# Ten dense matmuls of a recurrent step: two runs of five instead of five short runs

## The chip, the cores and the metric

The kernel runs on one core of a Trainium2 chip. The metric is the time of one execution on the device in microseconds; lower is better.

## The reference

The reference is one layer of a bidirectional encoder for two sequences (1024 and 512 tokens, width 1024), all in float32, with shared weights:

- RMSNorm, then one input projection `u = h @ w_in`. Its columns feed two groups of heads: an RWKV-7 time mixer (8 heads of 64, two directions) and an HGRN2 mixer (4 heads of 128, two directions).
- The RWKV-7 mixer is a recurrence over tokens. The state of each head is a 64 x 64 matrix, `S = S * w + (S @ -kk) b^T + v k^T`, and the output is `y = S @ r`.
- The HGRN2 mixer is a gated linear recurrence in chunks of 32 tokens. Its inputs q, f (two directions), i and g are 20 column tiles of 128 of `u`.
- Both outputs through one output projection, residual, RMSNorm, a mixture of experts (one of 4 groups, then 2 of 8 experts), residual, final RMSNorm.

## The kernel before

The kernel is a row of stages: `norm_in`, `project_rwkv` (the RWKV columns of `u`), **`mix_rwkv_project_hgrn`** (the fused stage, which the change touches), `mix_hgrn`, `mixer_out`, `route`, `experts`, `combine`. Each stage writes one instruction stream for each engine by hand, in program order, with semaphores between them. An engine does its stream strictly in that order, so a wait holds everything behind it. In the code `dve` is VectorE, `act` ScalarE, `pe` TensorE, `sp` the queue that issues most DMAs, `pool` GpSimd.

The fused stage does two jobs at once. One is the RWKV-7 recurrence in 48 chunks of 32 tokens, in both directions at a time. Three chunks are in flight: in a step of number `it`, chunk `a = it` is at its front, `b = it - 1` in the middle, `c = it - 2` at its back. There are 50 steps; 46 of them have all three. The other job is the projection of the HGRN2 columns: 60 units (20 column tiles, 3 spans of 512 tokens) of 8 dense 128x128x512 matmuls each. `project(it, lo, hi)` issues dense matmuls `lo` to `hi` of the ten that belong to a step (L968), so that 48 steps have dense work. Units take turns in two PSUM tiles `pp`, which ScalarE evicts; for the q columns `project` also does four transposes (L976) in the middle of a later unit.

The small groups of TensorE in a step, 16 matmuls each unless said otherwise (each float32 matmul is two records in the profile, so a group of 16 has 32):

- `right(c)` L1008, L1013 (two times 16): the right-hand side R. It waits for the state of the chunk before, for O of the chunk before (ScalarE's copy of the outputs out of the same PSUM tile, L1163), and for the v tile.
- `power` 2, 3 and 4 for `b` and 0 and 1 for `a` (L993, L995, L998): the inverse of a 32x32 triangular matrix by repeated squaring. Between two powers VectorE adds, copies and transposes the result (function `grow` in VectorE's part, L1197, L1199, L1201). The marks `turn1` to `turn4` say that the transpose is done; power i waits for `turn i`, power 0 for `P0`, a transpose of `m0`.
- `solve(c)` L1022, L1025 (two times 16): the solution u and part of the outputs. ScalarE then copies u from PSUM in four pieces (L1137).
- `scores(a)` L985: scores of the new chunk; VectorE masks them, ScalarE makes `m0` of them.
- `grow(c)` L1034, L1038 (two times 16), the function of TensorE's part: growth of the state and the rest of the outputs. It waits for the copies of u. VectorE then makes the new state (L1259, L1262).

TensorE's order in a step was: `right`, 3 dense, power 2, `solve`, `scores`, 2 dense, `grow`, power 3, 2 dense, power 0, 2 dense, power 4, 1 dense, power 1. The last dense matmul and the first three of the next step are parted by power 1 and `right` only. VectorE's order in a step was: work after power 2, masks, state (after `grow`), P0, work after power 3, after power 0, after power 4, after power 1, then what the projection needs of it. ScalarE's order in a step: R, copies of u, copies of the keys, `m0`, logarithms and exponentials of the HGRN2 gates in some steps, O, and evictions of the dense units between them.

## Time and profile before

| | us |
|---|---|
| median of 3 runs | 2946.04 (2942.31 to 2947.09) |
| the profiled execution: its own time | 2947.06 |
| its span, first to last instruction | 2945.3 |
| the fused stage, first dense matmul to last output copy | 592.18 to 1409.50, 817.32 |
| TensorE busy in the stage | 799.61 |
| VectorE busy in the stage | 376.28 |
| ScalarE busy in the stage | 342.79 |

Over the whole span TensorE is busy 82%, VectorE 39%, ScalarE 25%; the mean granted clock of TensorE is 0.891 of 2.4 GHz, in the fused stage 0.98. TensorE is the engine that is almost always busy in this stage, so the table is to be read together with the order of time inside a step: which engine releases TensorE's next group, and how far ahead of time.

### The profile page before, as it was taken

The numbers are of one execution on the slowest core, as the hardware profiler recorded it, in microseconds if no ns is written. First come the engines' busy times: TensorE is split into PE (matmuls) and PEld (weight loads), VectorE is DVE, ScalarE is ACT, GpSimd is POOL, SyncE is SP. The second block draws the span as 40 slices with busy tenths as digits, with TensorE's granted clock in tenths as the row PEclk, the third lists the DMA queues.
The fourth block names the chain that finished last, engine by engine and source line by source line (L and its number), as shares of the span: only waits on it lengthen the run. The fifth ranks groups of instructions, "written<-read, shape, count | busy, mean of one in ns | idle before, by whom it ended". The sixth has DMA issues, their size and how long they took to land. (4 is left out here: it accounts for less than half of the span.)

```text
span 2945.3 us, 64059 instructions
## 1 busy us (share of the span) xinstructions
PE 2405.8 (82%) x27916; PEld 1521.8 (52%) x27916; DVE 1135.2 (39%) x2034; ACT 726.5 (25%) x1362; POOL 198.3 (7%) x272
## 2 busy tenths in 40 slices
PE   3999999499999999999794266884199999999970
PEld 2434333155555555555693023342187888788850
DVE  3128776724634535436552654523010000000006
ACT  3124434423533534435111111110001011011002
POOL 0002111300000000000000000000300100011000
PEclk9999889599999999999796577887599999999985
DMA  3103333423433333332455233325378888888848
GB/s 86 48 8 106 122 103 120 152 69 77 113 83 79 111 83 86 97 83 64 138 157 192 76 110 107 112 81 115 108 302 327 328 327 311 326 330 325 315 154 323
DMA packets 348914, 460.45 MB, mean 156 GB/s; under 512 B 170272, under 2 KB 269200, under 8 KB 340496
## 3 DMA queue, kind: packets, MB, share of 16 engines
q1 hardware_dynamic: 338128, 421.87, 43.4%
q0 software_dynamic: 10560, 35.22, 3.0%
q8 instruction: 184, 3.01, 0.4%
q14 instruction: 42, 0.34, 0.0%
HBM read 348.52 MB, written 108.48 MB: 155 GB/s over the span
## 5 line engine op out<-in xcount | busy, mean ns | idle before, releaser
L968 PE MATMUL m_ps_pp<-hT,h_wcol 128*128 128x512 f32 x960 | 481.9, 623 | 24.2 <-DVE m_decay L1183 24.2
L421 PE MATMUL r_pp<-hT,r_wcol 128*128 128x512 f32 x720 | 314.0, 597 | 14.9 <-DMA r_wcol<-in_w_in_dram 14.6
L968 PEld LDWEIGHTS m_ps_pp<-hT,h_wcol 128*128 128x128 f32 x960 | 163.3, 190 | 158.8 <-issue 120.7
L2146 PEld LDWEIGHTS e_ps_g<-e_xT,e_wg 128*128 128x128 f32 x2048 | 235.6, 193 | 16.3 <-issue 16.3
L2156 PE MATMUL e_ps_y<-e_wd,e_hid 128*128 128x512 f32 x512 | 227.3, 597 | 12.9 <-DVE e_hid L2190 12.9
L2146 PE MATMUL e_ps_g<-e_xT,e_wg 128*128 128x128 f32 x2048 | 235.9, 276 | 1.1 <-DVE e_xT L2185 1.1
L2146 PE MATMUL e_ps_u<-e_xT,e_wu 128*128 128x128 f32 x2048 | 233.9, 275 | 0.0
L421 PEld LDWEIGHTS r_pp<-hT,r_wcol 128*128 128x128 f32 x720 | 137.5, 192 | 185.5 <-issue 185.5
L2146 PEld LDWEIGHTS e_ps_u<-e_xT,e_wu 128*128 128x128 f32 x2048 | 231.3, 192 | 0.0
L2190 DVE TENSOR_TENSOR e_hid<-e_ps_u,e_silu 128x512 f32<-128x512 f32 x32 | 22.1, 692 | 443.5 <-PE e_ps_u L2146 443.5
L1667 PE MATMUL o_ps_out<-o_wout,o_y 128*128 128x512 f32 x384 | 179.0, 627 | 0.0
L2156 PEld LDWEIGHTS e_ps_y<-e_wd,e_hid 128*128 128x128 f32 x512 | 94.7, 190 | 125.2 <-issue 125.2
L1667 PEld LDWEIGHTS o_ps_out<-o_wout,o_y 128*128 128x128 f32 x384 | 78.2, 205 | 101.9 <-issue 99.3
L1137 ACT ACTIVATE m_v<-m_ps_x 32x256 f32<-32x256 f32 x192 | 71.9, 374 | 177.3 <-PE m_ps_x L1025 175.6
L2193 DVE COPY e_y<-e_ps_y 128x512 f32<-128x512 f32 x32 | 22.1, 692 | 217.7 <-PE e_ps_y L2156 217.7
L2136 PE MATMUL e_ps_t<-ident,e_x 128*128 128x128 f32 x264 | 35.7, 279 | 80.8 <-DMA e_x<-h,e_idx 80.8
L2168 ACT ACTIVATE e_xT<-e_ps_t 128x512 f32<-128x512 f32 x33 | 19.7, 597 | 305.6 <-PE e_ps_t L2136 305.6
L1751 DVE RECIPROCAL o_rt<-o_rt 128x512 f32<-128x512 f32 x24 | 80.4, 3348 | 1.5 <-ACT o_rt L1701 0.7
L1649 PE MATMUL o_ps_mean<-o_of,headsum 128*128 128x512 f32 x24 | 23.9, 1099 | 66.0 <-DVE o_of L1728 66.0
L2136 PEld LDWEIGHTS e_ps_t<-ident,e_x 128*128 128x128 f32 x264 | 32.7, 192 | 81.9 <-issue 81.9
L1189 DVE TENSOR_TENSOR m_sm<-m_ps_s,m_mask 128x256 f32<-128x256 f32 x96 | 40.0, 424 | 90.1 <-PE m_ps_s L985 67.0
L2176 ACT ACTIVATE e_y<-e_ps_y 128x512 f32<-128x512 f32 x32 | 19.1, 597 | 219.8 <-PE e_ps_y L2156 219.8
(310 smaller groups left out, 3319.9 us busy)
## 6 DMA issues: line engine op xcount, KB each, us to landing
e_wg<-in_moe_w_gate_dram SPq DMA_DIRECT2D x32, 2048.0 KB, 8.0
e_wu<-in_moe_w_up_dram SPq DMA_DIRECT2D x32, 2048.0 KB, 12.5
e_wd<-in_moe_w_down_dram SPq DMA_DIRECT2D x32, 2048.0 KB, 13.1
ar<-r_ar SPq DMA_DIRECT2D x24, 512.0 KB, 2.7
kb<-r_kb SPq DMA_DIRECT2D x24, 512.0 KB, 2.7
m_ar<-ar SPq DMA_DIRECT2D x48, 256.0 KB, 4.4
m_kb<-kb SPq DMA_DIRECT2D x48, 256.0 KB, 3.5
kq<-h_kqst SPq DMA_DIRECT2D x24, 512.0 KB, 4.2
```

What stands on the lines that cost most here:

```text
L421: last = nc.tensor.matmul(pp[s][:], wcol[q][:, c], self.hT[:, c, s * SPAN:(s + 1) * SPAN], start=c == 0, stop=c == KT - 1)
L968: last = nc.tensor.matmul(pp[n % 2][:], wcol[k % 3][:, c], self.hT[:, c, span(s)], start=c == 0, stop=c == KT - 1)
L1137: last = nc.scalar.activation(out, ps_ru[quad[q]], ACT.Copy)
L1189: nc.vector.tensor_tensor(by_dir(sm[a % RING][:, w::2]), by_dir(ps_s[:, w, :, 0:2 * CH]), mask[:].unsqueeze(2).broadcast_to((P, 2, 2, 2 * ...
L1649: nc.tensor.matmul(ps_mean[:], self.headsum[:], of[u][:], start=True, stop=True).then_inc(*pe_r.inc("mean"))
L1667: last = nc.tensor.matmul(ps_out[:, half * SPAN:(half + 1) * SPAN], y[:, k, t * P:(t + 1) * P], wout[:, k, half * SPAN:(half + 1) * SPAN], ...
L1751: nc.vector.reciprocal(rt[u][:], rt[u][:]).then_inc(*dve_n.inc("inv"))
L2136: last = nc.tensor.transpose(ps_t[:, c * P:(c + 1) * P], x[u][:, c:D:KT], self.ident[:])
L2146: last = nc.tensor.matmul(ps[:, q * P:(q + 1) * P], w[u][:, c, q * P:(q + 1) * P], xT[u][:, c * P:(c + 1) * P], start=c == 0, stop=c == KT ...
L2156: last = nc.tensor.matmul(ps_y[:, n * 512:(n + 1) * 512], hid[u][:, q * P:(q + 1) * P], wd[u][:, q, n * 512:(n + 1) * 512], start=q == 0, ...
L2190: nc.vector.tensor_tensor(hid[u][:], ps_u[:], silu[:], ALU.mult).then_inc(*dve.inc("hid"))
L2193: nc.vector.tensor_copy(y[u][:, 512:], ps_y[:, 512:]).then_inc(*dve.inc("y"))
```

## The change

On TensorE, the ten dense matmuls of a step are issued as two runs of five. Power 2 moves ahead of the first run, power 3 ahead of `grow`, and power 0, power 4 and power 1 stand side by side after the second run, followed by `right` and power 2 of the next step. On VectorE, the work after power 3 moves ahead of the new state. No instruction is added or taken away.

```diff
                         if has_c:
                             right(c)
-                        project(it, 0, 3)
                         if has_b:
                             self.waits(eng, dve_a.at("turn2", b))
                             power(ps_b, b % 2, 2).then_inc(*pe_b.inc("I2"))
+                        project(it, 0, 5)
                         if has_c:
                             solve(c)
                         if has_a:
                             scores(a)
-                        project(it, 3, 5)
-                        if has_c:
-                            grow(c)
                         if has_b:
                             self.waits(eng, dve_b.at("turn3", b))
                             power(ps_b, b % 2, 3).then_inc(*pe_b.inc("I3"))
-                        project(it, 5, 7)
+                        if has_c:
+                            grow(c)
+                        project(it, 5, 10)
                         if has_a:
                             self.waits(eng, dve_a.at("P0", a))
                             power(ps_a, a % 2, 0).then_inc(*pe_a.inc("I0"))
-                        project(it, 7, 9)
                         if has_b:
                             self.waits(eng, dve_b.at("turn4", b))
                             power(ps_b, b % 2, 4).then_inc(*pe_b.inc("I4"))
-                        project(it, 9, 10)
                         if has_a:
                             self.waits(eng, dve_a.at("turn1", a))
                             power(ps_a, a % 2, 1).then_inc(*pe_a.inc("I1"))
...
                             masked(a, 1)
+                        if has_b:
+                            self.waits(eng, pe_b.at("I3", b))
+                            grow(dve_b, ps_b, b, 4)
                         if has_c:
...
-                        if has_b:
-                            self.waits(eng, pe_b.at("I3", b))
-                            grow(dve_b, ps_b, b, 4)
                         if has_a:
                             self.waits(eng, pe_a.at("I0", a))
                             grow(dve_a, ps_a, a, 1)
```

TensorE in the fused stage before, from power 1 of one step to power 3 of the next (a row is a line, its operation, tile written <- tiles read, the moving tile, and a count; `m_ps_a` and `m_ps_b` are the powers of chunks a and b, `m_ps_pp` the dense units):

```order
L995 MATMUL m_ps_a<-m_px,m_pw 32x64 x16
L1008 MATMUL m_ps_x<-m_v,m_sm 32x64 x16
L1013 MATMUL m_ps_x<-m_state,m_ar 32x64 x16
L968 MATMUL m_ps_pp<-hT,h_wcol 128x512 x3
L995 MATMUL m_ps_b<-m_px,m_pw 32x64 x16
L1022 MATMUL m_ps_x<-m_rs,m_xt 32x64 x16
L1025 MATMUL m_ps_x<-m_ar,m_state 64x32 x16
L985 MATMUL m_ps_s<-m_ar,m_kb 64x128 x16
L968 MATMUL m_ps_pp<-hT,h_wcol 128x512 x2
L1034 MATMUL m_ps_x<-m_v,m_kbt 64x64 x16
L1038 MATMUL m_ps_x<-m_sm,m_v 64x32 x16
L995 MATMUL m_ps_b<-m_px,m_pw 32x64 x16
```

The same place now, from power 0:

```order
L993 MATMUL m_ps_a<-m_m,m_pw 32x32 x16
L998 MATMUL m_ps_b<-m_px,m_pw 32x32 x16
L995 MATMUL m_ps_a<-m_px,m_pw 32x64 x16
L1008 MATMUL m_ps_x<-m_v,m_sm 32x64 x16
L1013 MATMUL m_ps_x<-m_state,m_ar 32x64 x16
L995 MATMUL m_ps_b<-m_px,m_pw 32x64 x16
L968 MATMUL m_ps_pp<-hT,h_wcol 128x512 x5
L1022 MATMUL m_ps_x<-m_rs,m_xt 32x64 x16
L1025 MATMUL m_ps_x<-m_ar,m_state 64x32 x16
L985 MATMUL m_ps_s<-m_ar,m_kb 64x128 x16
L995 MATMUL m_ps_b<-m_px,m_pw 32x64 x16
L1034 MATMUL m_ps_x<-m_v,m_kbt 64x64 x16
```

Power 0 (L993), 4 (L998), 1 (L995 of `m_ps_a`), `right` and power 2 follow each other without a dense matmul between them, and so do solve, scores, power 3 and `grow`.

VectorE before, from the masks of a step to the work after power 0 (`m_ps_b` rows belong to power 3, the line `m_grown` to the state):

```order
L1189 TENSOR_TENSOR m_sm<-m_ps_s,m_mask 128x4x64 x2
L1259 TENSOR_TENSOR m_grown<-m_ps_x,m_state 128x2x4x64
L1262 TENSOR_TENSOR m_state<-m_grown,m_decay 128x512
L1267 STREAM_TRANSPOSE m_pw<-m_m 128x128
L1268 TENSOR_TENSOR m_px<-m_m,m_eye 128x4x32
L1197 TENSOR_TENSOR m_px<-m_px,m_ps_b 128x4x32
L1199 COPY m_px<-m_ps_b 128x4x32
L1201 STREAM_TRANSPOSE m_pw<-m_px 128x128
L1199 COPY m_px<-m_ps_a 128x4x32
```

The same place now (its lines stand three higher up to the masks, L1189 is L1186):

```order
L1186 TENSOR_TENSOR m_sm<-m_ps_s,m_mask 128x4x64 x2
L1194 TENSOR_TENSOR m_px<-m_px,m_ps_b 128x4x32
L1196 COPY m_px<-m_ps_b 128x4x32
L1198 STREAM_TRANSPOSE m_pw<-m_px 128x128
L1259 TENSOR_TENSOR m_grown<-m_ps_x,m_state 128x2x4x64
L1262 TENSOR_TENSOR m_state<-m_grown,m_decay 128x512
L1267 STREAM_TRANSPOSE m_pw<-m_m 128x128
L1268 TENSOR_TENSOR m_px<-m_m,m_eye 128x4x32
L1196 COPY m_px<-m_ps_a 128x4x32
```

The three instructions after power 3 moved ahead of the two of the state and of P0.

## Rows read from the trace of the kernel before

**Rows 1.** The page, groups of instructions: busy us, mean ns | idle us before it
```profile
L968 PE MATMUL m_ps_pp<-hT,h_wcol 128*128 128x512 f32 x960 | 481.9, 623 | 24.2 <-DVE m_decay L1183 24.2
```

**Rows 2.** Windows (us): busy us and (x) records of each engine, clock, DMA share, GB/s
```profile
1005.59:1021.89 16.30, 16.30 (x411) 9.46 (x404) 8.21 (x24) 5.92 (x16) 0.00 (x0) 1.00 0.39 110
1153.82:1172.76 18.94, 16.58 (x425) 9.60 (x418) 11.25 (x31) 12.89 (x23) 0.00 (x0) 1.00 0.45 113
1172.76:1189.06 16.30, 16.30 (x408) 9.45 (x413) 10.61 (x27) 10.15 (x20) 0.00 (x0) 1.00 0.30 100
969.99:987.83 17.84, 17.84 (x408) 10.35 (x412) 10.61 (x27) 10.19 (x20) 0.00 (x0) 0.91 0.26 87
969.95:973.30 3.35, 3.35 (x66) 2.09 (x67) 3.28 (x7) 1.55 (x2) 0.00 (x0) 0.50 0.92 329
1372.79:1390.57 17.78, 17.78 (x408) 10.30 (x412) 10.61 (x27) 10.14 (x20) 0.00 (x0) 0.91 0.21 72
```

**Rows 3.** TensorE's waits, 600 to 1390: us in total, times, longest
```profile
PE m_ps_x L1008 <- issue: 9.4, 4, 2.4
```

**Rows 4.** Order of time (start, us, engine line, tiles), TensorE, one step
```profile
1005.98 2.84 PE L968 MATMUL m_ps_pp<-hT,h_wcol 128*128 128x512 f32 x6
...
1008.75 0.65 PE L995 MATMUL m_ps_b<-m_px,m_pw 32*32 32x64 f32 x32
...
1009.17 0.52 PEld L1022 LDWEIGHTS m_ps_x<-m_rs,m_xt 32*32 32x32 f32 x32
...
1009.78 1.06 PE L1025 MATMUL m_ps_x<-m_ar,m_state 64*64 64x32 f32 x30
...
1011.74 1.98 PE L968 MATMUL m_ps_pp<-hT,h_wcol 128*128 128x512 f32 x4
...
1013.65 0.69 PE L1034 MATMUL m_ps_x<-m_v,m_kbt 64*64 64x64 f32 x32
...
1014.71 0.65 PE L995 MATMUL m_ps_b<-m_px,m_pw 32*32 32x64 f32 x32
...
1015.29 1.98 PE L968 MATMUL m_ps_pp<-hT,h_wcol 128*128 128x512 f32 x4
...
1017.21 0.45 PE L993 MATMUL m_ps_a<-m_m,m_pw 32*32 32x32 f32 x32
...
1017.59 1.98 PE L968 MATMUL m_ps_pp<-hT,h_wcol 128*128 128x512 f32 x4
...
1020.94 0.59 PE L995 MATMUL m_ps_a<-m_px,m_pw 32*32 32x64 f32 x27
...
1021.32 0.21 PE L1008 MATMUL m_ps_x<-m_v,m_sm 32*32 32x64 f32 x1
```

**Rows 5.** The same step, ScalarE and VectorE
```profile
1010.95 1.53 ACT L1137 ACTIVATE m_v<-m_ps_x 32x256 f32<-32x256 f32 x4 [4.39 <-PE m_ps_x L1025]
...
1017.74 0.29 DVE L1199 COPY m_px<-m_ps_a 128x128 f32<-128x128 f32 x1 [0.33 <-PE m_ps_a L993]
...
1018.06 0.31 DVE L1201 STREAM_TRANSPOSE m_pw<-m_px 128x128 f32<-128x128 f32 x1
```

**Rows 6.** Order of time, the last steps of the stage
```profile
1390.14 0.59 PE L995 MATMUL m_ps_a<-m_px,m_pw 32*32 32x64 f32 x27
...
1391.75 0.65 PE L995 MATMUL m_ps_b<-m_px,m_pw 32*32 32x64 f32 x32 [0.20 <-DVE m_pw L1201]
...
1392.77 1.12 PE L1025 MATMUL m_ps_x<-m_ar,m_state 64*64 64x32 f32 x32
...
1393.94 1.53 ACT L1137 ACTIVATE m_v<-m_ps_x 32x256 f32<-32x256 f32 x4 [1.88 <-PE m_ps_x L1025]
...
1395.53 0.69 PE L1034 MATMUL m_ps_x<-m_v,m_kbt 64*64 64x64 f32 x31 [1.63 <-ACT m_v L1137]
```

**Rows 7.** Order of time around one late O
```profile
969.48 0.36 ACT L1163 ACTIVATE m_oacc<-m_ps_x 128x256 f32<-128x256 f32 x1
...
969.94 1.08 PE L1008 MATMUL m_ps_x<-m_v,m_sm 32*32 32x64 f32 x32 [2.36 <-issue]
```

## The prediction

> **What bounds the kernel now.** I read the groups of instructions first, then busy time by stretch, then the waits, and last the order of time inside one step. The groups show that the dense matmuls of the fused stage are 481.9 us of TensorE [rows 1], the costliest line of the program; the change moves just these. The windows show one ordinary step of the stage, from the second half of one `right` to that of the next: 16.30 us, and TensorE is busy for all of them at the full 2.4 GHz [rows 2]. So in an ordinary step nothing but TensorE's own queue sets the time: every microsecond of idle that a new order brings is paid, and every drain that it saves is a gain. Four of the 48 `right` groups are an exception: TensorE waits before them, 9.4 us in all [rows 3]. These steps take 18.94 us [rows 2], because ScalarE, 12.89 us busy, is late with its copy of the outputs (O), which `right` waits for: O starts at 969.48, `right` at 969.94 (the row names no releaser, only "issue"; O's end is the last event before it) [rows 7].
>
> **What five runs cost now.** All starts in this paragraph are in [rows 4]. A dense matmul is two records. Six records take 2.77 us until the next small group (1005.98 to 1008.75), four take 1.91 (1011.74 to 1013.65), so a record is 0.43 us and entering a small group from a dense run costs about 0.20 on top. A 32x64 group is 0.42 us when another 32-row group follows (1008.75 to 1009.17, power 2 before solve) and 0.58 when a dense run follows (1014.71 to 1015.29, power 3), so leaving costs 0.16. Each dense run thus costs some 0.36 us beyond its matmuls. A step has five and will have two: 1.1 us fewer. Part of it comes back, since small groups of different tile shapes stand side by side where a dense run parted them (`right` before power 2, scores before power 3), at about that 0.16 to 0.19 each time.
>
> **What stood in the shade of the runs.** The small groups form chains through VectorE and ScalarE, and a dense run after a group is what covers the answer. Three of the covers go.
>
> 1. *power 0 to power 1.* Power 1 needs turn 1, which VectorE makes from power 0. Power 0 starts at 1017.21 [rows 4], the copy at 1017.74, the transpose at 1018.06 and it ends at 1018.37 [rows 5]; a group that waits begins 0.06 us after its release (u ends at 1393.94 + 1.53 = 1395.47, `grow` starts at 1395.53 [rows 6]). That is 1.22 us from power 0 to power 1. Before, six records and power 4 lay between (3.73 us, 1017.21 to 1020.94). Now only power 4 does; power 0 takes 0.38 with a dense run behind it, 0.22 without the leaving, and power 4 is alike: about 0.5 us for both. Wait: 0.7.
> 2. *power 1 to power 2.* Same chain, with the addition in front. The last steps of the stage have no dense run left and show it bare: power 1 at 1390.14, power 2 at 1391.75, released by VectorE's transpose [rows 6]: 1.61 us. `right`, which lies between, covers all but some 0.25.
> 3. *solve to grow.* ScalarE copies u out of PSUM in four pieces, 1.53 us, beginning 1.17 after solve's second half (1009.78 [rows 4], 1010.95 [rows 5]); the last steps show the whole way, 1392.77 to 1395.53: 2.76 us [rows 6]. In between now stand solve's second half and scores (1009.78 to 1011.74 is 1.96 [rows 4]) and power 3 with a change of shape, 0.58: 2.54. Wait: 0.2.
>
> The VectorE edit (turn 4's work ahead of the state's) goes with power 3 moving ahead of `grow`. I cost it at nothing: power 3's answer is then worked on while `grow` runs, and both the state and P0 have a dense run of 4.5 us as cover; without the edit only that cover would be shorter.
>
> **The sum of an ordinary step.** Along TensorE's queue, from [rows 4] and [rows 6]:
> - two dense runs of ten records: 2.77 + 4 x 0.43 = 4.49 each, 8.98
> - power 0 to power 1 1.22; power 1 to power 2 1.61; power 2 into the dense run, as power 3 now, 0.58
> - solve's first half 0.61 (1009.17 to 1009.78); its second half to `grow` 2.76; `grow` 1.06 (1013.65 to 1014.71)
>
> Together 16.82 against 16.30: **0.52 us slower**, the 0.68 won on drains less 1.2 of waits. There are 46 steps with all three chunks in flight: 23.9 us.
>
> **The four heavy steps.** O hangs on ScalarE, which there works without a pause from u on, so its time after solve stays. Solve's second half to `right` is 1009.78 to 1021.32 = 11.54 us now [rows 4], and will be 2.76 + 1.06 + 4.49 + 1.22 + 0.38 = 9.91. TensorE therefore arrives 1.63 earlier and waits 1.63 longer, about 4.0 instead of 2.35 (9.4 / 4 [rows 3]); power 2's own 0.25 is then free. 1.38 x 4 = 5.5 us. The wait has a second price. After one such idle of 2.36 us the first small group started at 969.94 [rows 7], and the stretch from 969.95 ran at a granted clock of 0.50, which is 1.2 GHz [rows 2]; the step took 17.84 where the like step after 1172.76, at 1.00, took 16.30 [rows 2]. So a fall costs 1.54. It happened after two of the four: the steps from 969.99 and 1372.79 show 0.91, and the one from 1172.76, at 1.00, stands for the other two [rows 2]. With 4 us of idle I count four: 2 x 1.54 = 3.1 us.
>
> **The rest.** The first two steps have no `right` and few small groups; power 1 and power 2 wait there too, nearly bare: 1.4 us together, an estimate from the 1.22 and 1.61. Evictions of the dense tiles and DMA loads cost nothing: none of TensorE's waits in the stage is for them [rows 3], and between two uses of a buffer now always lies a small stretch of 3.4 us or more. If that cover failed, it would be by less than one eviction, a few times.
>
> Sum: 23.9 + 5.5 + 3.1 + 1.4 = 33.9 us. The profiled execution took 2947.06, so 2981; it stands 1.0 above the median of the runs shown, so **2980**.
>
> Bounds for an ordinary step: the drains could be won in full (1.1), or the waits be 0.3 longer, since power 4 and power 2 follow each other more closely on VectorE: +0.3 to +0.8. With 46 steps and a clock term of 0 to 6 us that is 2964 to 2998, the forecast's own range.
>
> **Rivals.**
> - *The drains win (faster).* Place: the three borders of small groups above. If the waits come to less than 0.68 us a step, fewer borders decide. With none, a step is 15.6, 46 x -0.68 = -31, and the heavy steps, where TensorE arrives another 1.2 earlier, give back some 10: 2926. For it: 13 changes of shape a step become 9, and each costs 0.16 to 0.20 in [rows 4]. Against it: power 2 and `grow` wait openly in [rows 6] at just the intervals of my sum, and neither engine in those chains is busy with other things there. Chance 0.08. The Trainium skill (TensorEngine Tiling, Key Properties) says that a change of tiling mode, not of tile alone, drains TensorE; by that rule the new order gains. The trace agrees in kind, and gives the size.
> - *The orders balance.* Both terms near 0.7 to 0.9: 2940 to 2952. Chance 0.05. That the change does not do what it says I leave out: the instruction order shows the runs of five.
> - *The clock falls in the small stretches.* The longest stretch without a dense matmul is now 1008.75 to 1011.74, 2.99 us, gapless [rows 4]. It becomes 1.22 + 1.61 + 0.58 = 3.41 with nearly 1 us of idle in it, and 4.43 with 0.2. If little work in a stretch is enough for the fall, it comes in some steps, not all: in one of three, 16 x 1.54 = 25 us more, 3005 (chance 0.13); in each, 71 us and more, over 3050 (0.04). For it: the fall at 969.95 came after no full standstill but after a small group and 2.36 us idle [rows 2, 7]. Against it: the last steps from 1390.14 to 1392.77 are small groups with a wait inside [rows 6] and their records keep their lengths. The Trainium skill (TensorE: Matmul & The Clock Gate, the two states) lets the clock fall after idleness alone; by it this rival would be worth nothing.
>
> **Chances.** Forecast 0.70, the clock rival 0.17, balance 0.05, faster 0.08. About 0.2%, 5.9 us, is what can be told from no change. Slower 0.87, same 0.05, faster 0.08. The range leaves out the faster rival, the balance and the clock falling in each step: 0.17; it reaches from just under the forecast's own to past the one-in-three case: 2962 to 3010.
>
> **What would show it.** In the profile after, an ordinary step should be near 16.8 us; power 1 and power 2 should be released by VectorE's transpose and `grow` by ScalarE's copy of u, each in 40 steps or more, with about 0.7, 0.25 and 0.2 us; the wait before `right` should be 4 us four times, with half clock after each. I am wrong if these waits are missing, if steps are below 16.3, or if the clock stands at 0.50 in ordinary steps.

## The result and the profile after

| | before | after |
|---|---|---|
| median of 4 runs each, us | 2945.18 (2942.31 to 2947.09) | 3006.47 (3003.06 to 3011.18) |
| span of the profiled execution | 2945.3 | 3009.4 |
| the fused stage, first dense matmul to last output copy | 817.2 | 878.1 |
| an ordinary step, undisturbed | 16.30 | 16.78 |
| the median of all 47 steps | 16.30 | 17.48 |

The change makes the kernel slower by 2.1% (ratio 1.021, 95% interval 1.0192 to 1.0228), about 61 us. That is 26 us above the predicted number, above the forecast's own range of 2964 to 2998, and inside the wider range of 2962 to 3010. The whole of it lies in the fused stage: 878.1 - 817.2 = 60.9.

The page's groups first: the dense matmuls, and ScalarE's copies of u (which stood at L1137).

```profile
L968 PE MATMUL m_ps_pp<-hT,h_wcol 128*128 128x512 f32 x960 | 453.8, 619 | 24.7 <-DVE m_decay L1180 24.4
...
L1134 ACT ACTIVATE m_v<-m_ps_x 32x256 f32<-32x256 f32 x192 | 71.8, 374 | 274.1 <-PE m_ps_x L1025 272.4
```

The 960 matmuls are as many as in [rows 1]. Their busy time is even lower, 453.8 against 481.9 (I put that down to the overlap of records at the borders of a run, of which there are fewer). So the work did not grow; what grew is the time in which TensorE stands still: 878.13 - 803.42 = 74.7 us in the stage now, 817.32 - 799.61 = 17.7 before. The windows show it (us; then busy us and records of TensorE's matmuls, its loads, VectorE, ScalarE, GpSimd; granted clock, DMA share, GB/s). In this order they are: an ordinary step, a heavy step, the step after it, the first 6.6 us of that, 3.4 us after a pause, a step with a pause, and the stage.

```profile
966.58:983.36 16.78, 15.96 (x419) 9.70 (x411) 10.83 (x29) 5.35 (x15) 0.00 (x0) 1.00 0.19 42
983.36:1004.42 21.06, 16.41 (x428) 9.98 (x416) 12.32 (x33) 12.89 (x23) 0.00 (x0) 0.99 0.49 121
1004.42:1023.96 19.54, 18.87 (x396) 11.31 (x400) 9.15 (x25) 10.37 (x20) 0.00 (x0) 0.83 0.18 64
1004.30:1010.90 6.60, 6.43 (x101) 3.88 (x102) 5.28 (x13) 1.74 (x3) 0.00 (x0) 0.50 0.46 174
659.40:662.80 3.40, 3.40 (x23) 1.75 (x24) 0.80 (x3) 0.00 (x0) 0.00 (x0) 0.51 0.51 140
841.36:859.59 18.23, 16.25 (x419) 9.82 (x411) 6.77 (x20) 4.64 (x13) 0.00 (x0) 1.00 0.36 98
593.05:1471.18 878.13, 803.42 (x19440) 488.60 (x19440) 365.93 (x1062) 340.01 (x772) 0.00 (x0) 0.97 0.30 79
```

Compare with [rows 2]. The ordinary step is 16.78 instead of 16.30, and TensorE is busy for 15.96 of it where it was busy for all. The heavy step is 21.06 instead of 18.94, and the step after it 19.54 at a clock of 0.83, where before it was 17.84 at 0.91 or 16.30 at 1.00. The step from 841.36 has no such wait and no low clock, and yet takes 18.23.

TensorE's waits between 598 and 1450 (us in total, times, longest) say which answers it waits for:

```profile
PE m_ps_a L995 <- DVE m_pw L1198: 22.4, 47, 0.8
PE m_ps_x L1008 <- issue: 15.8, 4, 4.0
PE m_ps_b L995 <- issue: 8.2, 11, 1.2
PE m_ps_b L995 <- DVE m_pw L1198: 8.0, 37, 1.0
PE m_ps_x L1013 <- issue: 3.8, 3, 1.3
PE m_ps_x L1034 <- ACT m_v L1134: 2.0, 13, 0.2
```

Power 1 (`m_ps_a`) waits 47 times for VectorE's transpose, 22.4 / 47 = 0.48 us by the record; power 2 (`m_ps_b`, released by VectorE) 37 times 0.22; `grow` (L1034) 13 times 0.15 (this view lists only idle time above 0.15 us; the trace has 0.14 or 0.15 us before `grow` in 45 of 50 steps); `right` (L1008) four times 3.95, where [rows 3] had four times 2.35. These are the predicted waits (for power 1 I had written 0.7 and counted in it the leaving of power 4, which the record of power 4 hides here). But there are two lines that I had not expected: 11 waits in an `m_ps_b` group and 3 in the second half of `right` (L1013) that end with "issue", that is, with nothing that another engine did. The order of time shows what they are (start, us, engine line, tiles; idle before in brackets):

```profile
841.04 0.59 PE L995 MATMUL m_ps_a<-m_px,m_pw 32*32 32x64 f32 x27 [0.47 <-DVE m_pw L1198]
...
842.65 0.64 PE L995 MATMUL m_ps_b<-m_px,m_pw 32*32 32x64 f32 x28 [0.20 <-DVE m_pw L1198]
844.44 0.30 PE L995 MATMUL m_ps_b<-m_px,m_pw 32*32 32x64 f32 x4 [1.16 <-issue]
844.67 4.56 PE L968 MATMUL m_ps_pp<-hT,h_wcol 128*128 128x512 f32 x10
849.16 0.65 PE L1022 MATMUL m_ps_x<-m_rs,m_xt 32*32 32x64 f32 x32
849.74 1.06 PE L1025 MATMUL m_ps_x<-m_ar,m_state 64*64 64x32 f32 x30
...
851.69 0.65 PE L995 MATMUL m_ps_b<-m_px,m_pw 32*32 32x64 f32 x32
852.49 0.70 PE L1034 MATMUL m_ps_x<-m_v,m_kbt 64*64 64x64 f32 x32
...
853.56 4.56 PE L968 MATMUL m_ps_pp<-hT,h_wcol 128*128 128x512 f32 x10
858.05 0.45 PE L993 MATMUL m_ps_a<-m_m,m_pw 32*32 32x32 f32 x32
858.32 0.48 PE L998 MATMUL m_ps_b<-m_px,m_pw 32*32 32x32 f32 x32
859.27 0.59 PE L995 MATMUL m_ps_a<-m_px,m_pw 32*32 32x64 f32 x27 [0.47 <-DVE m_pw L1198]
```

Power 2 begins at 842.65 after its wait for VectorE. Then 28 of its 32 records are done, TensorE stands still for 1.16 us, and the last four come at 844.44. No semaphore lies between the 28th and the 29th record. I call this a **pause**.

A late O looks as in [rows 7], with a longer wait (ScalarE, then TensorE):

```profile
1004.01 0.36 ACT L1160 ACTIVATE m_oacc<-m_ps_x 128x256 f32<-128x256 f32 x1
...
1004.47 1.08 PE L1008 MATMUL m_ps_x<-m_v,m_sm 32*32 32x64 f32 x32 [3.87 <-issue]
```

### The profile page after: what moved, and what is told of

Same layout as the page of the kernel before. It is cut to its first block and busy times, and to the rows that moved or that the text cites. A ratio compares the mean times of both kernels' runs of the same rounds, so it can differ in the third digit from the quotient of the medians.

```text
span 3009.4 us, 64059 instructions
## 1 busy us (share of the span) xinstructions
PE 2414.0 (80%) x27916; PEld 1547.8 (51%) x27916; DVE 1125.0 (37%) x2034; ACT 723.7 (24%) x1362; POOL 198.3 (7%) x272
## 5 line engine op out<-in xcount | busy, mean ns | idle before, releaser
L968 PE MATMUL m_ps_pp<-hT,h_wcol 128*128 128x512 f32 x960 | 453.8, 619 | 24.7 <-DVE m_decay L1180 24.4
L968 PEld LDWEIGHTS m_ps_pp<-hT,h_wcol 128*128 128x128 f32 x960 | 179.3, 196 | 219.8 <-issue 188.3
L1186 DVE TENSOR_TENSOR m_sm<-m_ps_s,m_mask 128x256 f32<-128x256 f32 x96 | 40.7, 425 | 295.2 <-PE m_ps_s L985 267.1
L995 PE MATMUL m_ps_b<-m_px,m_pw 32*32 32x64 f32 x3072 | 68.4, 224 | 19.1 <-DVE m_pw L1198 10.7
L1196 DVE COPY m_px<-m_ps_a 128x128 f32<-128x128 f32 x96 | 27.6, 287 | 139.9 <-PE m_ps_a L993 139.9
```

The source lines that it names most:

```text
L968: last = nc.tensor.matmul(pp[n % 2][:], wcol[k % 3][:, c], self.hT[:, c, span(s)], start=c == 0, stop=c == KT - 1)
L995: last = nc.tensor.matmul(ps[q, j, 0:2 * CH], pw[u][q, j], px[u][q, j], start=True, stop=True)
L1186: nc.vector.tensor_tensor(by_dir(sm[a % RING][:, w::2]), by_dir(ps_s[:, w, :, 0:2 * CH]), mask[:].unsqueeze(2).broadcast_to((P, 2, 2, 2 * ...
```

## Where the 61 us are

The steps are taken one by one, from each `right` to the next; a pause is an idle stretch that lies inside one group.

- *Ordinary steps*: 46 x 0.48 = 22 us.
- *Heavy steps*: 21.06 - 18.94 - 0.48 = 1.64 each, 6.6 us.
- *Pauses*: 16, of 0.35 to 1.30 us, 13.5 us together (before: 2, 1.3 us). The step with the pause of 1.16 us is 18.23 - 16.78 = 1.45 longer. In the twelve steps with a pause, no late O and no low clock, the excess is 0.02 to 0.45 us more than the gap, 0.23 on average: 13.5 + 16 x 0.23 = 17 us, of which some 2 were there before. About 15 us, an estimate.
- *Clock*: the stage's steps have 8 stretches at half clock (the granted clock reads 0.50, 1.2 GHz), 41 us together; before it was 2 with 6.8 us. Four come with a late O and last 6.83 us each; the step with one is 19.54 - 16.78 = 2.8 longer (the last one, which begins 1.9 us before `right`, only 18.74 - 16.78 = 2.0), where one of 3.41 us before cost 1.54. Four come among the small groups between power 0 and power 2 (at 608.3, behind a wait for VectorE, and at 659.5, 765.3 and 949.6, each within 0.5 us of the end of a pause), and last 3.41 us. By these step lengths 3 x 2.8 + 2.0 + 3 x 1.5 - 2 x 1.5 = 12 us, the one at 608.3 being in the next line.
- *First steps*: the first `right` comes 29.5 us after the first dense matmul instead of 26.7: 2.8 us.
- *The end*: the last `right` waits 0.94 us, where it did not before: 0.9 us.

That is 22 + 6.6 + 15 + 12 + 2.8 + 0.9 = 59 of 61 us. Of the 27 us that the forecast lacks, some 15 are pauses and 9 the clock (12 less the 3.1 that it had).

Every one of the 16 pauses resumes at the same place in TensorE's program. Counted from its first instruction in the trace, it is number 97 in a block of 256. The DMA records of the queue that the page calls "instruction" have their counterpart (transfers, MB, share of 16 engines):

```profile
q8 instruction: 184, 3.01, 0.4%
```

These are 16 KB each; 153 of them start in the stage, and TensorE crosses 153 borders between blocks of 256 there. Before the pause that ends at 844.44 one such transfer started at 841.56 and took 1.45 us; before that which ends at 862.05 one started at 859.23 and took 1.43. In all 16 TensorE resumes 1.26 to 1.54 us after the transfer landed. So my reading was, before the runs of the section on pauses: TensorE's program is fetched in blocks of 256 instructions, a 32-row group of 16 float32 matmuls is 64 loads and matmuls in 0.42 us, and where enough such groups stand side by side TensorE reaches the end of a block before the next one has come. In a dense run of ten records the same engine needs 4.49 us for 20 instructions, and the fetch catches up. The Trainium skill (Runtime: NRT & Kernel Launch, Instruction fetch mechanics) also has blocks of 256 instructions and 16 KiB, and says that fetching is hidden because issue is slower than filling. The trace agrees with the block and not with the hiding.

## The experiments

Each kernel was compared with the kernel before on the same chip. In the table the plain step, the waits before `right` for O, the pauses and the low clock are counted in each trace in the same way (the waits for VectorE in the first steps are no pauses; the drained end is left out of the clock). "Plain step" is the length of the undisturbed steps. "Longest" is the longest stretch of small groups without a dense matmul, in loads and matmuls. Pauses, clock and steps come from the one profiled execution of each kernel. Pauses are those inside a group; one more, which ends with the first instruction of the next group, is in the kernel before (0.31 us), in it with O first (0.41), and in the five kernels from the changed one to power 1 behind `right` except the one with more instructions ahead (0.29 to 0.56).

| kernel | median us | ratio, 95% | plain step | O waits | longest | pauses | half clock |
|---|---|---|---|---|---|---|---|
| before | 2945.18 | | 16.30 | 4 x 2.4 | 256 | 2, 1.3 us | 2, 6.8 us |
| after | 3006.47 | 1.0192 to 1.0228 | 16.78 | 4 x 4.0 | 384 | 16, 13.5 | 8, 41 |
| power 2 behind the run | 2970.73 | 1.0080 to 1.0123 | 16.38 | 4 x 3.9 | 448 | 8, 5.9 | 4, 24 |
| VectorE's order as before | 2998.66 | 1.0168 to 1.0211 | 16.8 | 4 x 4.0 | 384 | 17, 13.4 | 4, 20 |
| 128 more instructions ahead | 3010.05 | 1.0209 to 1.0246 | 16.79 | 4 x 4.0 | 384 | 15, 8.0 | 4, 27 |
| power 0 inside the run | 2966.35 | 1.0059 to 1.0100 | 16.40 | 4 x 4.3 | 384 | 5, 4.7 | 5, 24 |
| power 1 behind `right` | 2968.11 | 1.0057 to 1.0100 | 16.08 | 4 x 5.0 | 448 | 8, 8.4 | 6, 31 |
| after, O first | 2974.40 | 1.0083 to 1.0133 | 16.79 | none | 384 | 21, 13.9 | none |
| power 1 behind `right`, O first | 2947.13 | 0.9995 to 1.0017 | 16.08 | none | 448 | 13, 10.0 | 1, 3 |
| before, O first | 2929.93 | 0.9933 to 0.9964 | 16.30 | none | 256 | 1, 0.7 | none |
| four runs | 2934.06 | 0.9962 to 0.9987 | 16.06 | 4 x 2.5 | 256 | 1, 0.2 | 3, 14 |
| four runs, O first | 2920.75 | 0.9905 to 0.9932 | 16.06 | none | 256 | 2, 0.7 | none |
| the same, power 4 behind power 0 | 2916.57 | 0.9892 to 0.9922 | 16.02 | none | 256 | none | none |
| that, power 3 behind scores | 2925.27 | 0.9923 to 0.9956 | 16.02 | none | 320 | 4, 3.3 (+ 2, 3.9) | 2, 10 |

### One part of the change at a time

**Power 2 behind the run.**

```diff
                             right(c)
+                        project(it, 0, 5)
                         if has_b:
...
                             power(ps_b, b % 2, 2).then_inc(*pe_b.inc("I2"))
-                        project(it, 0, 5)
```

> Power 2 stands behind the first dense run again, all else as in the changed kernel. Theory of the waits: the wait of power 2 (0.24) and one change of shape go, a plain step falls from 16.78 to about 16.4 us, that is 17 us over 46 steps; the 0.7 before power 1 and the 0.2 before grow stay. Theory of the instruction supply (in the changed kernel TensorE pauses 17 times, 13.9 us, in the middle of a small group, each time at the same place modulo 256 of its instruction stream): the stretch from power 0 to the first run has a group less, so its pauses get fewer, those between solve and grow may get more; with fewer pauses there the clock falls less often. Together 20 to 35 us below the changed kernel, 2972 to 2986. If only the waits count: 2989.

Measured 2970.73, just under the expected range. The plain step is 16.38: the wait of power 2 and one change of shape are gone. The pauses are half as many. The stretch from power 0 to the first run has one group fewer (320), but that from power 2 to `grow` one more (448), so the length of the longest stretch alone doesn't give their number.

**VectorE's order as before**, TensorE's changed.

```diff
                             masked(a, 1)
-                        if has_b:
-                            self.waits(eng, pe_b.at("I3", b))
-                            grow(dve_b, ps_b, b, 4)
                         if has_c:
...
+                        if has_b:
+                            self.waits(eng, pe_b.at("I3", b))
+                            grow(dve_b, ps_b, b, 4)
                         if has_a:
                             self.waits(eng, pe_a.at("I0", a))
```

> The changed kernel with the VectorE edit undone (the work after power 3 stands behind the new state and P0 again). My theory: nothing, within 3 us of the changed kernel, since the answer to power 3 is needed only after a dense run of 4.5 us. Rival (the edit carries part of the loss or of the gain, by delaying the state or turn 4): 10 us or more either way.

Measured 2998.66. The plain step, the waits and the pauses are those of the changed kernel. The 8 us less, where at most 3 were expected, go with four stretches at half clock instead of eight, 20 us instead of 41. The VectorE edit by itself is nothing in a step, as predicted; whether it has to do with which idle stretches are followed by a low clock, one profiled execution doesn't tell.

**Power 0 inside the second run**, so that runs are 5, 3 and 2.

```diff
-                        project(it, 5, 10)
+                        project(it, 5, 8)
...
                             power(ps_a, a % 2, 0).then_inc(*pe_a.inc("I0"))
+                        project(it, 8, 10)
```

> Power 0 stands inside the second run, three dense matmuls before it and two behind (runs of 5, 3, 2). Theory of the waits: the 0.7 us before power 1 go, one more run costs 0.36, a plain step is 16.44 instead of 16.78, 16 us in all, 2990. With the supply and the clock: the longest stretch of small groups is a group and a wait shorter, so some pauses and some falls of the clock go too: 2970 to 2985. If the 0.7 was not the price: no gain, or 10 us slower by the extra run.

Measured 2966.35, 40 us below the changed kernel and 4 below the expected range, with one run more. The waits of power 1 are gone from the trace (of 47 none is left), and the step is 16.40: 0.38 less. So a wait of 0.7 us was bought with one border of some 0.36: 17 of the 40 us. The rest goes with fewer pauses (5 instead of 16) and less time at half clock (24 us instead of 41).

**Power 1 behind `right`**, with its own work on VectorE moved accordingly: the other way to cover power 0's answer, with two runs kept.

```diff
                             right(c)
                         if has_b:
+                            self.waits(eng, dve_a.at("turn1", b))
+                            power(ps_a, b % 2, 1).then_inc(*pe_a.inc("I1"))
+                        project(it, 0, 5)
+                        if has_b:
...
                             power(ps_b, b % 2, 2).then_inc(*pe_b.inc("I2"))
-                        project(it, 0, 5)
...
-                            power(ps_a, a % 2, 1).then_inc(*pe_a.inc("I1"))
```

> The changed kernel with power 1 of a chunk behind right of the next step, and power 2 behind the first dense run (VectorE's work after power 1 stands first in its step). Two runs of five stay. Theory: power 4 and right now fill the time from power 0 to power 1, a dense run the time from power 1 to power 2; a plain step falls to 15.83 us, 0.47 below the kernel before: the drains won with one wait of 0.2 before grow. The four heavy steps wait for O even longer (some 5 us each, with a fall of the clock after each), which takes back 12 plus 9, and pauses of the instruction supply some 5: 2935 to 2955. Rival (fewer runs win nothing by themselves, only waits changed): plain step 16.3, 2965 or more.

Measured 2968.11, a miss by 13 us. The step is 16.08 and not 15.83. TensorE, in order of time, power 0, power 4 and `right` side by side:

```profile
791.30 0.45 PE L993 MATMUL m_ps_a<-m_m,m_pw 32*32 32x32 f32 x32
791.58 0.48 PE L998 MATMUL m_ps_b<-m_px,m_pw 32*32 32x32 f32 x32
792.02 0.65 PE L1008 MATMUL m_ps_x<-m_v,m_sm 32*32 32x64 f32 x32
```

Power 4 takes 0.44 us until `right` starts, where I had reckoned with 0.25, power 4 without the leaving of a dense run. The waits between 600 and 1390 tell of the rest:

```profile
PE m_ps_x L1008 <- ACT m_oacc L1160: 15.3, 3, 5.1
PE m_ps_x L1008 <- issue: 4.8, 1, 4.8
PE m_ps_a L995 <- issue: 4.5, 3, 1.6
PE m_ps_b L995 <- issue: 2.7, 4, 2.0
```

TensorE arrives still earlier, so each late O costs 5 us, and seven waits that only "issue" ends come to 7.2 us.

### The late O and the clock

**The changed kernel with O first**: ScalarE copies the outputs ahead of the logarithms and exponentials of the step instead of behind them.

```diff
+                        if has_c:
...
+                            nc.scalar.activation(by_way(oacc[c // 4 % 2])[:, :, :, c % 4 * CH:(c % 4 + 1) * CH], ps_o,
+                                                 ACT.Copy).then_inc(*act_c.inc("O"))
                         for m in range(2 * PAIRS):
...
                                 decays(m)
-                        if has_c:
...
-                            nc.scalar.activation(by_way(oacc[c // 4 % 2])[:, :, :, c % 4 * CH:(c % 4 + 1) * CH], ps_o,
-                                                 ACT.Copy).then_inc(*act_c.inc("O"))
```

> The changed kernel with ScalarE's copy O ahead of the logarithms and exponentials in its stream. Theory: the four waits before right (16 us) and the clock's falls behind them (some 3 us each) go, plain steps stay at 16.8 and power 1, power 2 and grow wait as before, pauses stay: 22 to 28 us below the changed kernel, 2978 to 2985. If the clock fell for other reasons: only 13 us below, 2993.

Measured 2974.40, 32 us below the changed kernel, more than expected. TensorE's waits between 600 and 1430:

```profile
PE m_ps_a L995 <- DVE m_pw L1198: 22.9, 48, 0.8
PE m_ps_b L995 <- DVE m_pw L1198: 11.3, 42, 2.5
PE m_ps_b L995 <- issue: 8.7, 12, 1.2
PE m_ps_x L1034 <- ACT m_v L1134: 7.1, 46, 0.2
```

No line with L1008 for O is left, and not one stretch of the stage's steps is at half clock. The waits of powers 1 and 2 and the pauses are all still there. So the late O caused 4 x 4.0 us of waiting and, with what follows it, most of the clock's share. The four falls among the small groups went as well, though the pauses did not (21 of them); a pause alone thus doesn't bring a fall each time.

**The kernel before with the same edit.**

> The kernel before with O ahead of the logarithms and exponentials alone. Theory: its four waits (9.4 us) and two falls (3 us) go: 2932 to 2937. It says how much of the seventh kernel's gain is the order of ScalarE. If something else in the heavy steps is late next: nothing, 2944.

Measured 2929.93, 15.7 us faster than the kernel before measured beside it (2945.60), 2 us more than expected, and faster than both kernels. An ordinary and a formerly heavy step (columns as above), and O beside TensorE in order of time:

```profile
945.57:961.88 16.31, 16.31 (x420) 9.47 (x412) 8.93 (x25) 10.33 (x20) 0.00 (x0) 1.00 0.43 106
961.88:978.17 16.29, 16.29 (x420) 9.46 (x412) 12.82 (x32) 12.61 (x24) 0.00 (x0) 1.00 0.43 126
```

```profile
973.24 0.38 ACT L1154 ACTIVATE m_oacc<-m_ps_x 128x256 f32<-128x256 f32 x1
...
973.64 1.28 ACT L1117 ACT_TABLE_LOAD   x1
...
978.22 0.21 PE L1008 MATMUL m_ps_x<-m_v,m_sm 32*32 32x64 f32 x1
```

O is copied at 973.24, and `right` needs it at 978.22. ScalarE is as busy as it was (12.61 us), and the step is 16.29 instead of 18.94: it was the order on ScalarE and not its load that made these steps heavy.

**Power 1 behind `right`, and O first**, both diffs together.

> Both: power 1 behind right, power 2 behind the first run, and O ahead of the logarithms and exponentials. Theory: plain steps of 15.83, no wait for O, no fall of the clock: 21 us below before by the plain steps, 6 by the heavy ones (four steps of 16.9 instead of 18.94 and others), 3 by the clock, 5 to 10 given back in pauses of the instruction supply: 2918 to 2928, below both kernels.

Measured 2947.13, level with before (ratio 1.0006), a miss of some 20 us. The O waits are gone, the step is 16.08 instead of the expected 15.83 (46 x 0.25 = 11.5 us), the last two steps take 34.1 us instead of the 26.8 of the kernel before (a pause of 1.67 us, 3.41 us at half clock and a wait of power 2 for VectorE of 3.9 us lie in them), and 13 pauses take 10 us. `grow` still waits for the copies of u, 38 times, 5.8 us together. Two runs without the waits of power 1 and power 2 in ordinary steps and without the late O thus only reach what five runs have.

### The pauses

**128 more instructions ahead of the stage.** The loop increments a semaphore that nobody waits for, and shifts all blocks of 256 by half a block.

```diff
+                    for _ in range(128):
+                        eng.sem_inc(shifted, 1)
                     for c, has_a, has_b, has_c in steps():
```

> The changed kernel with 128 semaphore increments more on TensorE's queue ahead of the fused stage's first step. Theory of the instruction supply: the pauses in the middle of small groups stay at multiples of 256 instructions and so come 128 instructions earlier in the order of the work, in other groups and other steps; their number may change (10 to 25), and with it the time by up to 15 us. Rival (the pauses belong to the work: a late load, a busy memory, an eviction): the same groups of the same steps pause as in the changed kernel, near 659, 765, 844, 862 us of the span, and the time is within 3 us.

Measured 3010.05. The increments themselves take 19.5 us ahead of the stage (591.05 to 610.57); the stage is 863.3 against 878.1, with 8.0 us of pauses instead of 13.5 and 27 us at half clock instead of 41. The pauses all lie at other places: counted from the first `right`, the first three are in the steps 1, 5 and 6 and no longer in 3, 8 and 9, and where a step has one in both kernels (three do) it is in another group. They are still at number 97 of a block, the increments counted. They hang on the place in the program, not on the operation or on data. This excludes a semaphore, PSUM or DMA wait of the kernel as their cause.

**Four runs of 3, 2, 3, 2.** This takes the useful half of the idea: one border fewer, no group with a chain behind another that it depends on, and no stretch over 256 instructions.

```diff
-                        project(it, 5, 7)
+                        project(it, 5, 8)
...
                             power(ps_a, a % 2, 0).then_inc(*pe_a.inc("I0"))
-                        project(it, 7, 9)
+                        project(it, 8, 10)
...
                             power(ps_b, b % 2, 4).then_inc(*pe_b.inc("I4"))
-                        project(it, 9, 10)
```

> The kernel before with the dense matmuls of a step in four runs (3, 2, 3, 2) instead of five, and power 1 at the end of the step's groups, behind power 4. If one run less is worth what the plain steps of the other runs show (a change of matmul kind and its drain, 0.2 to 0.36 us a step) and no wait appears for a decayed window or an output copy, the plain step is 15.95 to 16.15 us against 16.30, and with the pauses and late O matmuls of before the time is 2932 to 2940. If putting power 4 beside power 1 costs the 0.17 us that it cost in the run with power 1 behind `right`, the plain step is about 16.1 and the time at the upper end. Rival: more small groups side by side bring the pauses in the middle of a group (over 8 of them, where before has 2) and falls of the clock (over 3): 2945 or more.

Measured 2934.06, 8.9 us below the kernel before measured beside it (2942.98), as expected: the step is 16.06, the pauses are as rare as before, and the heavy steps are 18.94 as before, which eats what is won in them.

**The same with O first.**

> The same order of the groups, with the copy of O ahead of the logarithms and exponentials on ScalarE. It took 15.6 us from the kernel before and all of its falls of the clock; the same gain on top of four runs gives 2915 to 2925, with no wait for O and no fall. Rival: pauses in the middle of groups come instead, 2930 or more.

Measured 2920.75, inside the expected range, with no wait for O and no fall of the clock.

**The same with power 4 behind power 0**, and the run of two between power 4 and power 1.

> As the run with four runs and outputs first, but power 4 directly behind power 0, and the two dense matmuls between it and power 1. If it matters only how many runs there are, within 3 us of that run. If two small groups side by side cost as such, the one with power 4 beside power 0 (0.42 us for power 4 where it is 0.25 alone) is as dear as the one with power 4 beside power 1, again within 3 us; a plain step of over 0.1 us difference would say that it matters which groups meet.

Measured 2916.57, **the fastest of all** by its median: 26 us below the kernel before measured beside it (2942.98), 0.9907 of it (its interval and that of the run before it overlap). A step (window, then TensorE in order of time):

```profile
1101.35:1117.38 16.03, 16.03 (x420) 9.51 (x412) 6.60 (x20) 9.52 (x19) 0.00 (x0) 1.00 0.32 78
```

```profile
1111.66 2.84 PE L968 MATMUL m_ps_pp<-hT,h_wcol 128*128 128x512 f32 x6
1114.44 0.45 PE L993 MATMUL m_ps_a<-m_m,m_pw 32*32 32x32 f32 x32
1114.71 0.50 PE L998 MATMUL m_ps_b<-m_px,m_pw 32*32 32x32 f32 x32
1115.14 1.98 PE L968 MATMUL m_ps_pp<-hT,h_wcol 128*128 128x512 f32 x4
1117.05 0.59 PE L995 MATMUL m_ps_a<-m_px,m_pw 32*32 32x64 f32 x27
```

16.03 us and TensorE busy in all of it. Between power 0 (1114.44) and power 1 (1117.05) lie 2.61 us, twice the 1.22 of the chain. Here too power 4 takes 0.43 until the next work, so it doesn't matter which neighbour it has: the plain step is 0.04 us shorter. Of the 4 us between the two medians, where at most 3 were expected, 46 x 0.04 = 1.8 are explained by that; the rest I leave open.

**Power 3 behind scores**, the test of the fetch theory: from the fastest kernel one group is moved so that power 2, solve, scores and power 3 make a stretch of 320 instructions. Runs, changes of shape and covers stay.

```diff
                             scores(a)
+                        if has_b:
+                            self.waits(eng, dve_b.at("turn3", b))
+                            power(ps_b, b % 2, 3).then_inc(*pe_b.inc("I3"))
                         project(it, 3, 5)
                         if has_c:
                             grow(c)
-                        if has_b:
-                            self.waits(eng, dve_b.at("turn3", b))
-                            power(ps_b, b % 2, 3).then_inc(*pe_b.inc("I3"))
```

> The run with four runs and power 4 behind power 0, with one group moved: power 3 stands directly behind scores, ahead of the two dense matmuls, instead of behind grow. The number of dense runs, the changes of shape and all waits stay, but the longest stretch of small groups is now five groups of 16 (power 2, solve, scores, power 3: 320 loads and matmuls) instead of four (256). In the runs so far the pauses in the middle of a group came 0 to 2 times where the longest stretch was 256, and 6 to 22 times where it was 320 or more. If the length of the stretch decides, 4 or more pauses appear here, in power 3 or scores, and the time is 1 to 8 us above that run's 2916.57: 2918 to 2925. Rival: the pauses hang on the number of dense runs, or on waits between the small groups; then there are 0 to 2 and the time is within 2 us of that run.

Measured 2925.27, 8.7 us above, at the upper end of what was expected (the two intervals, 0.9892 to 0.9922 and 0.9923 to 0.9956, don't meet). The plain step is unchanged, 16.02. There are four pauses inside power 3 with 3.3 us, and two more just behind it, before a dense matmul, with 3.9 us; all six at number 97 of a block. The longest, TensorE in order of time, and the window after it:

```profile
980.59 0.65 PE L995 MATMUL m_ps_b<-m_px,m_pw 32*32 32x64 f32 x32
984.48 3.78 PE L968 MATMUL m_ps_pp<-hT,h_wcol 128*128 128x512 f32 x4 [3.24 <-issue]
```

```profile
983.60:989.00 5.40, 4.52 (x34) 1.99 (x37) 0.00 (x0) 0.00 (x0) 0.00 (x0) 0.50 0.03 9
```

Power 3 starts at 980.59 and the next instruction at 984.48, after 3.24 us with nothing to wait for, and the stretch behind it is at half clock. The profiled execution took 2930.59, the slowest of the four; the other three, 2923.76 to 2925.61, are still all above the fastest kernel's 2912.95 to 2919.01. One group of 64 instructions more in one stretch has brought the pauses back, with the number of dense runs the same. That settles it between my two theories. The table says the same over all kernels: with a longest stretch of 256, 0 to 2 pauses; with 320 or more, 4 to 21.

The traces show what a stretch of more than 256 brings. In every kernel with a stretch of 320 or more, each pause inside a group comes at the 294th to 433rd load or matmul of its stretch, which is behind the second block border in that stretch; a stretch of 256 has no second one. In the changed kernel 15 of the 16 transfers that TensorE paused for started 0.7 to 1.2 us after TensorE had crossed the border before (one 2.5), and TensorE went on 3.3 to 4.8 us after that border; without the gap it would have gone through the 256 instructions in 2.4 to 3.6 us. Some 28 other such borders of the changed kernel passed without a pause, so length makes pauses possible and doesn't fix their number. A late start counts as well. The few pauses of the kernels with 256 came at a first border, behind transfers that started 2.6 to 3.5 us after the border before, and the three long ones here (1.14, 1.77 and 3.24 us) behind 1.9, 2.7 and 4.1. What delays such a start no run shows, so the size of these three is not explained by the added group alone.

## Why the prediction was right, and where it wasn't

- **The ordinary step: right.** 16.82 forecast, 16.78 measured. The pieces agree too: a dense run of five 4.49 (844.67 to 849.16), power 0 to power 1 1.22 (858.05 to 859.27), power 1 to power 2 1.61 (841.04 to 842.65), solve's second half to `grow` 2.75 (849.74 to 852.49). All three waits appear with the releaser that was named. The view lists `grow`'s only 13 times because it leaves out idle time of up to 0.15 us; the trace has it in 45 of 50 steps, at 0.14 to 0.15 us where 0.2 was forecast (in the changed kernel with O first the view lists 46).
- **The heavy steps: right in kind.** The wait is 4.0 us four times as forecast. The step was to be 18.94 + 0.52 + 1.38 = 20.84 and is 21.06. The 0.25 of power 2 that I had taken off as free was not: it lies ahead of solve, and O's time hangs on solve. Nearly 1 us in all.
- **The time: in range, in part by luck.** 3006 is past the forecast's own 2998. The range went on to 3010 for a rival in which the clock falls in one step of three (3005), and that is not what happened: three falls among the small groups outside the first steps cost 4.5 us, and the largest part of the excess is pauses, which no term and no rival had.
- **The clock: the step that failed first.** "With 4 us of idle I count four" was right in number for the late O, and the size was wrong. I priced a fall by the one that followed 2.36 us of idle, 1.54; with 3.87 us of idle it lasted 6.83 us instead of 3.41 and cost 2.8. And there are four more falls with shorter idle stretches. 3.1 us forecast, about 12 found, 41 us at half clock instead of 6.8. The rival in which the clock falls in the small stretches was right in kind and not in size: four falls, not sixteen. The rule of the Trainium skill (TensorE: Matmul & The Clock Gate, the two states), by which that rival would be worth nothing, isn't borne out by this trace: the falls at 659.5 and 949.6 came behind gaps of 0.86 and 0.63 us among small groups. But 21 like gaps in the changed kernel with O first brought none, and what decides stays open.
- **The pauses: missing from the sum.** About 15 us. [Rows 4] show a gapless stretch of 2.99 us, and I took from it that small groups side by side run without a gap however many they are. The wait list of the kernel before had the hint in it, two waits ended by "issue" inside a group, 1.3 us together, which I had passed over.
- **The first steps**: 1.4 forecast, 2.8 found, with one fall of the clock among them.
- **The VectorE edit, evictions and DMA loads at nothing**: right. The run with VectorE's old order has the same plain step, and no wait of TensorE names an eviction or a load.
- **The rivals of the other sign** were rightly small. But the run with four runs shows what the drains are worth where no cover is lost: 0.24 to 0.28 us a step for one run less, 11 to 13 us in the stage.

## What to carry to other kernels

Count a border between dense and small matmuls against what the dense run covers: a border cost 0.24 to 0.36 us here, a chain of TensorE, VectorE and TensorE 1.2 to 1.6. Where such a chain exists, keep its two ends on both sides of a dense run, and merge only runs that cover nothing. Count the instructions in a stretch of small float32 matmuls as well as its time: here 256 loads and matmuls in a row gave 0 to 2 pauses in the stage, 320 or more 4 to 21. And look at the copy on another engine that frees PSUM for the bottleneck engine before anything else: putting four late copies ahead of work that nobody waited for was worth 15.7 us, four runs instead of five 8.9.

## What the runs showed of the hardware

- TensorE runs dry of instructions. It stands still for 0.15 to 1.98 us in the middle of a group and up to 3.24 us between two, each time at number 97 in a block of 256 instructions, and goes on 1.1 to 1.6 us after a transfer of 16 KB on the instruction queue has landed. These transfers take 0.88 to 2.2 us each in the stage. What decides when one starts is not shown.
- With the four late O of the changed kernel (3.9 to 4.0 us of idle) the clock was at 1.2 GHz for 6.83 us. In the kernel before (2.36 us of idle) it was 3.41 us twice and nothing twice, and in the other runs with waits of 2.2 to 5.1 us it was nothing, 3.41 or 6.83. It also fell behind gaps of 0.63 to 1.3 us among small groups, four times in the changed kernel, and behind pauses of 1.2 to 3.2 us six times in four other kernels, but not once in the changed kernel with O first, which has more such gaps. What makes the difference is open.
- Power 0, a 32x32 group, takes 0.27 us when power 4 follows it (1114.44 to 1114.71), and power 4 takes 0.43 when a dense run follows and 0.44 when `right` does. Parted by a dense run each takes 0.38 (power 0: 1017.21 to 1017.59 [rows 4]; power 4, in the kernel before with O first: 976.40 to 976.78). So the pair saves 0.06 of its own, and the 0.20 of entering a small group from a dense run on top: 0.26, near the 0.24 to 0.28 a step that one run less brought.
- 128 semaphore increments on TensorE's queue took 19.5 us, 0.15 us each.
